# Splitting a depthwise convolution over three engines: one of its four channel tiles goes from VectorE to ScalarE and GpSimd

## The chip, the cores and the metric

One core of a Trainium2 chip runs the whole program in one launch. The metric is the device time of that core in microseconds (us), lower is better. A time is the median of several executions; a profile is one execution.

## What is computed

Two transformer-like layers over 128 context tokens and 256 latent tokens, held together as 384 columns. A layer normalises its input, multiplies it by one wide input projection, runs three token mixers on the result (a gated linear attention, a convolution module, a differential attention), merges them and runs a feed-forward part. The convolution module is the part that the change touches:

```
a, gate = jnp.split(u, 2, axis=-1)
y = a * jax.nn.sigmoid(gate)
y = lax.conv_general_dilated(y, w[:, None, :], window_strides=(1,), padding=[(CONV_PAD, CONV_PAD)],
                             dimension_numbers=('NWC', 'WIO', 'NWC'), feature_group_count=CONV_CH) + b
return jax.nn.silu(layernorm(y, ln_g, ln_b))
```

It has 512 channels and 31 taps a channel, and the layer norm behind it needs the sum over all channels.

## The kernel before

Every array is laid with channels on the 128 partitions and tokens along the free axis. All products with weights run on TensorE in three passes: a float32 weight tile is split into a high half (`w_hi`) and a remainder (`w_lo`), the activations likewise, and each tile takes high by high, high by low and low by high (L834 to L836). The weights come in pieces of 128 x 1024 values, 144 a layer; the input projection has pieces 0 to 57. For each piece SP (the queue that issues the loads) starts a load into `w_raw`, which has two buffers; ScalarE writes the high half (L1356), GpSimd subtracts and writes the low half (L703), and TensorE uses both. ScalarE's high half of piece s waits until TensorE is through with piece s-4, so ScalarE and GpSimd run up to four pieces ahead of it.

Each engine executes its instructions in the order in which they are written, and semaphores tie the engines together. There is no scheduler: what an engine does between two pieces is set by tables of piece numbers at the head of the file. `LEVEL_AT` gives the pieces behind which TensorE computes the seven doubling levels (0 to 6) and the two whole-tile rounds of the linear attention; `EXP_AT` the steps at which ScalarE exponentiates their factors; `SCORE_AT` the pieces behind which it does the scores of the twelve units (head, query tile) of the differential attention, unit 10 behind piece 51. `GATE_AT` and `EARLY_AT` place small products of the modulation vectors (L747) among layer 0's pieces.

For one level i VectorE builds the exponents (L1916 to L1921), copies the result of level i-2 out of PSUM under a mask in the middle of that (L1947), and, once ScalarE has exponentiated, multiplies (L1937). TensorE's level i (L940) needs the multiplication of i and the copy of level i-1, which stands in the build of i+1.

The convolution is done in float32 as 31 taps times four channel tiles (`CT` = 4), 124 instructions a layer, all on VectorE: tap w of tile ct is one 128 x 399 instruction `conv_acc = conv_in * cw + conv_acc` (L1803), where `conv_in` is read at an offset of w columns; the first tap of a tile has no accumulator to read (L1805). They have no place of their own. They are handed out as fillers by further tables: `LEVEL_TAPS` taps before the multiplication of each level from 2 on, `STATE_TAPS` and `OUT_TAPS` around the output of the linear attention, and in the differential attention `MAX_TAPS[u]` taps behind the row minimum of unit u and `WEIGHT_TAPS[u]` behind its weights. In unit 10 VectorE does all taps that are left, and then `conv_total`: three additions of the four tiles (L2022, L2024). Behind piece 53 TensorE sums that over the channels (`conv_mean`, L1094), before the values, transposes and scores that are next, and before piece 54. With the table of before, two taps are left when unit 10 begins, in either layer.

Of the kernel before, what the change touches and what calls it, by code (L numbers as in the profile page):

```python
# [28 lines left out]
P = 128  # L29
D = 1024  # L30
# [67 lines left out]
SECOND_LOAD = [1, 1, 1, 1, 1, 1, 1, 1]  # L98
SECOND_AT = [-1, -1, -1, 99, 99, 99, 99, 99]
GATE_LOAD = [5, 5, 5, 5, 6, 7, 8, 8]  # L100
GATE_AT = [5, 6, 6, 6, 6, 7, 8, 8]
EARLY_LOAD = [7, 8, 8, 9, 9, 14, 15, 15, 16, 16, 16, 18, 18, 21, 21, 22]
EARLY_AT = [11, 11, 11, 11, 11, 12, 12, 13, 16, 16, 16, 16, 17, 17, 18, 18]
TURN_AT_0 = [10, 16, 21]
TAKE_ACT_0 = [10, 17, 23]
PUT_ACT_0 = [14, 19, 24]
# [13 lines left out]
RSTD_ACT_0 = [34, 35, 36, 37]  # L120
PROMPT_KEYS_ACT_0 = 37
STATE_ACT_0 = 39
GLA_HI_ACT_0 = 42
SCORE_ACT_0 = [38, 39, 41, 43, 44, 46, 48, 49, 51, 53, 55, 57, 59, 61]

LEVEL_TAPS_0 = [0, 2, 8, 7, 4, 7, 7]
STATE_TAPS_0 = 15
OUT_TAPS_0 = [5, 6, 6, 1]
MAX_TAPS_0 = [1, 2, 2, 1, 2, 3, 1, 4, 0, 4, 5, 1]
WEIGHT_TAPS_0 = [2, 5, 3, 0, 6, 3, 2, 5, 6, 2, 6, 8]  # L130
BR0, WO0, FI0, FO0 = N_IN, N_IN + N_BR, N_IN + N_BR + N_WO, N_IN + N_BR + N_WO + N_FI
PIECES = FO0 + N_FO
assert PIECES % SPL == 0 and PIECES % RAW == 0
# [34 lines left out]
DECAY_ACT_1 = 10  # L168
SELF_ACT_1 = 11
TURN_AT_1 = [11]  # L170
TAKE_ACT_1 = [11]
PUT_ACT_1 = [15]
LEVEL_AT_1 = [10, 12, 13, 16, 17, 20, 21, 23, 26]
CACHE_KEYS_AT_1 = 23
ROTATE_AT_1 = [24, 26, 29, 30]
PROMPT_KEYS_AT_1 = 33
# [12 lines left out]
LEVEL_TAPS_1 = [1, 2, 6, 7, 1, 7, 10]  # L189
STATE_TAPS_1 = 16  # L190
OUT_TAPS_1 = [5, 6, 6, 1]
MAX_TAPS_1 = [1, 2, 2, 1, 2, 3, 1, 4, 0, 4, 6, 1]
WEIGHT_TAPS_1 = [2, 5, 3, 0, 6, 3, 2, 5, 6, 2, 6, 8]
# [56 lines left out]
def memory(nc):  # L250
# [104 lines left out]
def program(nc, x_prompt, x_sample, cache_diff_k, cache_diff_v, state_gla, c, c_ctx, w_mod, b_mod, norm1_g, norm2_g,  # L355
# [3 lines left out]
    with ExitStack() as ctx:  # L359
# [59 lines left out]

        pads = signal("pads", 3)  # L420
        y_prompt_ready = signal("y_prompt_ready", 2)
        tap = signal("tap", TAPS * CT)
        mean_done = signal("mean_done")
        centred = signal("centred", CT)
        csq = signal("csq", CT)
# [883 lines left out]
        def _(act):  # L1309
# [40 lines left out]
            for l in range(DEPTH):  # L1350
# [22 lines left out]
                def evacuate(c):  # L1373
# [14 lines left out]
                    elif c in (K_CG, K_CG + 1):  # L1388
                        fn(m["sq" if c == K_CG else "cg2"][:], src, ACT.Sigmoid).then_inc(done, 1)
                    elif c in (K_GG, K_GG + 1):  # L1390
                        if c == K_GG:
                            act.wait_ge(late_used.sem, late_at[l, 2, KD - 1] + 1)
                        fn(m["gg"][:, 2 * (c - K_GG):2 * (c - K_GG) + 2, :], src, ACT.Copy).then_inc(done, 1)
                    elif c in VALUES:
                        dst = m["gv" if c < K_DV else "dv"]
                        if c == K_DV + 1:
                            act.wait_ge(*keys_t.at(l, 1))
                        if VALUES[c]:
                            fn(dst[:, 2, :], ps[:, 2 * PAIR_OF[c], :], ACT.Copy).then_inc(done, 1)
                        else:  # L1400
                            fn(dst[:, 0:2, :], ps[:, 2 * PAIR_OF[c]:2 * PAIR_OF[c] + 2, :], ACT.Copy).then_inc(done, 1)
                    elif c < K_DV:
                        side, ht = (c - K_DQ) // 2, 2 * ((c - K_DQ) % 2)

                        fn(m["dqk"][:, side, ht:ht + 2, :], src, ACT.Copy, scale=1.0 if side else -DK ** -0.5).then_inc(done, 1)
                    else:
                        i = 2 * (c - K_GATE)
                        if i == 0:
                            act.wait_ge(early_used.sem, 2 * KD)
                        if i == 16:  # L1410
                            act.wait_ge(*o_mul.at(l, 2 * H))
                        if i + 1 >= 19:
                            act.wait_ge(*tap.at(l, TAPS * CT))
# [107 lines left out]
                for s in range(SPL, BR0 + 5):  # L1521
# [167 lines left out]
        def _(dve):  # L1689
# [52 lines left out]
            for l in range(DEPTH):  # L1742
# [52 lines left out]

                def taps(n):

                    for i in range(taps_done[0], min(taps_done[0] + n, TAPS * CT)):
                        w, ct = i // CT, i % CT
                        src, acc, wt = m["conv_in"][:, ct, w:w + AW], m["conv_acc"][:, ct, :], m["cw"][:, i:i + 1]  # L1800
                        if w:
                            dve.wait_ge(*tap.at(l, i - CT + 1))
# [3 lines left out]
                    taps_done[0] = min(taps_done[0] + n, TAPS * CT)  # L1806
# [249 lines left out]
                for u, (hh, q) in enumerate(UNITS):  # L2056
# [211 lines left out]
```

## Time and profile before

| | |
|---|---|
| median of 3 executions | 1441.1 us (1439.16 to 1444.92) |
| profiled execution | 1441.68 us, its span 1439.8 us |
| TensorE busy | 1395.1 us, 97% of the span |
| VectorE busy | 896.4 us, 62% |
| ScalarE busy | 603.9 us, 42% |
| GpSimd busy | 565.6 us, 39% |

Read it as a kernel with one full engine and three that prepare its operands. A busy time of VectorE or GpSimd is from start to end of an instruction, so it contains what the instruction waited inside. The granted TensorE clock is 0.992 of full over the span.

### The profile page before, as it was taken

To read this page: it belongs to the slowest core of one execution; us is meant where nothing else is said; L and a number is where in the kernel's file an instruction comes from. 1 tells how busy PE (TensorE), PEld (TensorE's weight loads), DVE (VectorE), ACT (ScalarE), POOL (GpSimd) and SP (SyncE) were. 2 spreads that over 40 slices of the span, in tenths; PEclk is the share of its full clock that TensorE was granted. 3 is DMA by queue.
4 is the path that set the end of the run, shared out by engine and by line. 5 is a ranking of instruction groups with operands and counts; after the bars stand their busy time and mean duration, and the time that the engine had idled before them with its cause. 6 is when DMAs were issued, how large, how long until landed. Compare 5 with 4: busy or idle time off the path is not lost.

```text
span 1439.8 us, 21521 instructions
## 1 busy us (share of the span) xinstructions
PE 1395.1 (97%) x8555; PEld 1315.1 (91%) x8555; DVE 896.4 (62%) x1122; ACT 603.9 (42%) x832; POOL 565.6 (39%) x237
## 2 busy tenths in 40 slices
PE   6999999999999999999999999999999999999998
PEld 3887998999998999999979889899999899999998
DVE  4559977995764488666565899698858432111022
ACT  3553434545734333332236344345464443333231
POOL 1353544444463100000025444444436545555552
PEclk9999999999999999999999999999999999999998
DMA  9865232433542766557424323243336434343441
GB/s 334 290 207 173 85 102 89 118 103 97 181 161 89 245 229 216 188 176 245 154 84 143 95 89 103 80 131 91 102 115 207 138 98 137 126 132 120 130 131 60
DMA packets 159212, 208.60 MB, mean 145 GB/s; under 512 B 9228, under 2 KB 126984, under 8 KB 159112
## 3 DMA queue, kind: packets, MB, share of 16 engines
q1 hardware_dynamic: 158560, 207.00, 44.9%
q8 instruction: 68, 1.11, 0.3%
q10 hardware_dynamic: 552, 0.22, 0.1%
q14 instruction: 32, 0.26, 0.1%
HBM read 204.05 MB, written 3.15 MB: 144 GB/s over the span
## 4 chain that ended last, share of the span: by engine, by line
PE 74%; DVE 11%; ACT 5%; DMA 4%; issue 2%; POOL 2%; SPq 1%; DVEq 0%; ACTq 0%; POOLq 0%
PE ps L834 22%; PE ps L836 21%; PE ps L835 21%; POOL w_lo L703 2%; DMA w_raw<-in_w_in_dram 1%; DVE conv_acc L1803 1%; ACT w_hi L1356 1%; DVE fac L1937 1%; DVE attn L1947 1%; DMA w_raw<-in_w_out_dram 1%; PE ps L1087 1%; PE ps L881 1%; DVE gates L2099 1%; DVE t L1762 1%; PE ps L882 1%
## 5 line engine op out<-in xcount | busy, mean ns | idle before, releaser
L703 POOL TENSOR_TENSOR w_lo<-w_raw,w_hi 128x1024 fp32r<-128x1024 f32 (+1 forms) x229 | 562.1, 2456 | 850.6 <-ACT w_hi L1356 728.5
L834 PE MATMUL ps<-h_hi,w_hi 128*128 128x384 f32 x1600 | 546.5, 342 | 6.5 <-DVE h_lo L1768 3.8
L836 PE MATMUL ps<-h_hi,w_lo 128*128 128x384 f32 x1600 | 535.7, 335 | 0.0
L835 PE MATMUL ps<-h_lo,w_hi 128*128 128x384 f32 x1600 | 535.6, 335 | 0.0
L1356 ACT ACTIVATE w_hi<-w_raw 128x1024 fp32r<-128x1024 f32 x199 | 207.6, 1044 | 434.2 <-PE ps L836 303.7
L834 PEld LDWEIGHTS ps<-h_hi,w_hi 128*128 128x128 f32 x1600 | 300.7, 188 | 21.7 <-issue 10.0
L835 PEld LDWEIGHTS ps<-h_lo,w_hi 128*128 128x128 f32 x1600 | 300.9, 188 | 1.4
L836 PEld LDWEIGHTS ps<-h_hi,w_lo 128*128 128x128 f32 x1600 | 300.8, 188 | 0.0
L1803 DVE SCALAR_TENSOR_TENSOR conv_acc<-conv_in,cw,conv_acc 128x399 f32<-128x399 f32 x240 | 210.7, 940 | 1.8
L1659 ACT ACTIVATE w_hi<-w_raw 128x1024 fp32r<-128x1024 f32 x88 | 93.2, 1061 | 211.4 <-PE ps L836 151.8
L834 PE MATMUL ps<-act_hi,w_hi 128*128 128x384 f32 x352 | 118.4, 336 | 0.0
L836 PE MATMUL ps<-act_hi,w_lo 128*128 128x384 f32 x352 | 117.6, 334 | 0.0
L835 PE MATMUL ps<-act_lo,w_hi 128*128 128x384 f32 x352 | 117.6, 334 | 0.0
L2139 DVE TENSOR_TENSOR w_lo<-w_raw,w_hi 128x1024 fp32r<-128x1024 f32 x59 | 72.2, 1224 | 64.1 <-ACT w_hi L1659 39.2
L2153 DVE TENSOR_TENSOR sq<-sq,ps 128x768 f32<-128x768 f32 x22 | 21.0, 952 | 141.7 <-PE ps L836 130.6
L1785 DVE SCALAR_TENSOR_TENSOR x<-ps,mod,x 128x128 f32<-128x128 f32 x32 | 11.2, 350 | 94.6 <-PE ps L836 94.5
L2128 DVE SCALAR_TENSOR_TENSOR mod_acc<-mod_late,cond,mod_acc 128x1024 f32<-128x1024 f32 x56 | 69.3, 1279 | 0.0
L834 PEld LDWEIGHTS ps<-act_hi,w_hi 128*128 128x128 f32 x352 | 66.1, 188 | 1.0 <-issue 0.8
L835 PEld LDWEIGHTS ps<-act_lo,w_hi 128*128 128x128 f32 x352 | 66.1, 188 | 0.1
L836 PEld LDWEIGHTS ps<-act_hi,w_lo 128*128 128x128 f32 x352 | 66.1, 188 | 0.0
L2156 DVE TENSOR_TENSOR act_lo<-sq,act_hi 128x768 fp32r<-128x768 f32 x22 | 38.5, 1751 | 13.6 <-ACT act_hi L1666 13.6
L881 PE MATMUL ps<-w_hi,h_hi 128*128 128x512 f32 x96 | 40.8, 425 | 3.1 <-DVE conv_in L1863 3.1
(262 smaller groups left out, 1656.4 us busy)
## 6 DMA issues: line engine op xcount, KB each, us to landing
w_raw<-in_w_in_dram SPq DMA_DIRECT2D x112, 512.0 KB, 3.6
w_raw<-in_w_ffn_in_dram SPq DMA_DIRECT2D x88, 512.0 KB, 3.5
mod_late<-in_w_mod_dram SPq DMA_DIRECT2D x71, 512.0 KB, 5.3
w_raw<-in_w_ffn_out_dram SPq DMA_DIRECT2D x44, 512.0 KB, 3.7
w_raw<-in_w_branch_dram SPq DMA_DIRECT2D x24, 512.0 KB, 3.4
mod_early<-in_w_mod_dram SPq DMA_DIRECT2D x16, 512.0 KB, 6.6
w_raw<-in_w_out_dram SPq DMA_DIRECT2D x16, 512.0 KB, 3.4
mod_second<-in_w_mod_dram SPq DMA_DIRECT2D x9, 512.0 KB, 11.1
```

The lines of the kernel that those rows point to most:

```text
L703: nc.gpsimd.tensor_tensor(m["w_lo"][:, n % SPL, cols], m["w_raw"][:, n % RAW, cols], m["w_hi"][:, n % SPL, cols].bitcast(F32), ALU.subtrac ...
L834: mm(out, hi[:, at:at + P], rhs[0][:, k, :], start=start, stop=False)
L835: mm(out, hi[:, at:at + P], rhs[1][:, k, :], start=False, stop=False)
L836: ins = mm(out, lo[:, at:at + P], rhs[0][:, k, :], start=False, stop=stop)
L881: mm(o, x[0], w[0], start=k == 0, stop=False)
L1356: fn(m["w_hi"][:, s % SPL, cols], m["w_raw"][:, s % RAW, cols], ACT.Copy).then_inc(hi_ready.sem, 1)
L1659: fn(m["w_hi"][:, s % SPL, :], m["w_raw"][:, s % RAW, :], ACT.Copy).then_inc(hi_ready.sem, 1)
L1803: v.scalar_tensor_tensor(acc, src, wt, acc, ALU.mult, ALU.add).then_inc(tap.sem, 1)
L2128: ins = v.scalar_tensor_tensor(acc, w, by, acc, ALU.mult, ALU.add)
L2139: v.tensor_tensor(m["w_lo"][:, s % SPL, :], m["w_raw"][:, s % RAW, :], m["w_hi"][:, s % SPL, :].bitcast(F32), ALU.subtract).then_inc(lo_re ...
L2153: v.tensor_tensor(m["sq"][:], m["sq"][:], pair[1], ALU.mult).then_inc(u_v.sem, 1)
L2156: v.tensor_tensor(m["act_lo"][:, 2 * i:2 * i + 2, :], m["sq"][:], m["act_hi"][:, 2 * i:2 * i + 2, :].bitcast(F32), ALU.subtract).then_inc( ...
```

## The change

The last channel tile (`VT` = 3) leaves VectorE. ScalarE multiplies tap w of it, behind the high half of piece 19 + w, into one of two new 128 x 399 buffers, `weighted`; GpSimd adds that to `conv_acc` behind the low half of piece 19 + w, for w from 1 to 30. The first tap ScalarE writes into `conv_acc` directly. VectorE keeps 31 taps of three tiles, 93 instead of 124 a layer, and its tables of taps hold smaller numbers. `conv_total` waits for GpSimd's last addition too. A few placements move: one modulation product of layer 0 from behind piece 5 to behind piece 6, two more one piece later, level 6 of layer 1 from behind piece 21 to behind piece 22, one read-out of ScalarE in layer 1 one step earlier, one copy of layer 0 one step earlier. The two buffers overlay columns of `gates` that are free until the gate chunks are read out, and ScalarE waits for the last addition before it writes there.

```diff
-GATE_AT = [5, 6, 6, 6, 6, 7, 8, 8]
+GATE_AT = [6, 6, 6, 6, 6, 7, 8, 8]
-EARLY_AT = [11, 11, 11, 11, 11, 12, 12, 13, 16, 16, 16, 16, 17, 17, 18, 18]
+EARLY_AT = [11, 11, 11, 11, 11, 12, 13, 13, 16, 16, 16, 16, 17, 17, 17, 18]
-GLA_HI_ACT_0 = 42
+GLA_HI_ACT_0 = 41
-LEVEL_TAPS_0 = [0, 2, 8, 7, 4, 7, 7]
+LEVEL_TAPS_0 = [0, 3, 5, 5, 3, 5, 5]
...
-MAX_TAPS_0 = [1, 2, 2, 1, 2, 3, 1, 4, 0, 4, 5, 1]
-WEIGHT_TAPS_0 = [2, 5, 3, 0, 6, 3, 2, 5, 6, 2, 6, 8]
+MAX_TAPS_0 = [1, 1, 1, 1, 2, 2, 0, 3, 0, 3, 3, 1]
+WEIGHT_TAPS_0 = [0, 4, 2, 0, 4, 2, 1, 4, 4, 1, 5, 5]
...
+TAP_FROM = 20
+VT = CT - 1
...
-LEVEL_AT_1 = [10, 12, 13, 16, 17, 20, 21, 23, 26]
+LEVEL_AT_1 = [10, 12, 13, 16, 17, 20, 22, 23, 26]
...
                 low(n)
+                w, layer = n % PIECES - TAP_FROM + 1, n // PIECES
+                if 1 <= w < TAPS:
+                    pool.wait_ge(*weighted.at(layer, w + 1))
+                    if w > 1:
+                        pool.wait_ge(*tap_p.at(layer, w - 1))
+                    acc = m["conv_acc"][:, VT, :]
+                    nc.gpsimd.tensor_tensor(acc, acc, m["weighted"][:, w % 2, :], ALU.add).then_inc(tap_p.sem, 1)
...
+                    w = s - TAP_FROM + 1
+                    if 0 <= w < TAPS:
+                        y = m["conv_in"][:, VT, w:w + AW]
+                        if w == 0:
+                            act.wait_ge(*evacuated(l, K_CA + 1))
+                            fn(m["conv_acc"][:, VT, :], y, ACT.Identity, bias=m["prm"][:, R_CB + VT:R_CB + VT + 1],
+                               scale=m["cw"][:, VT:VT + 1]).then_inc(weighted.sem, 1)
+                        else:
+                            if w >= 3:
+                                act.wait_ge(*tap_p.at(l, w - 2))
+                            fn(m["weighted"][:, w % 2, :], y, ACT.Copy, scale=m["cw"][:, w * CT + VT:w * CT + VT + 1]
+                               ).then_inc(weighted.sem, 1)
...
-                    for i in range(taps_done[0], min(taps_done[0] + n, TAPS * CT)):
-                        w, ct = i // CT, i % CT
+                    for i in range(taps_done[0], min(taps_done[0] + n, TAPS * VT)):
+                        w, ct = i // VT, i % VT
...
-                    dve.wait_ge(*tap.at(l, TAPS * CT))
+                    dve.wait_ge(*tap.at(l, TAPS * VT))
+                    dve.wait_ge(*tap_p.at(l, TAPS - 1))
```

GpSimd, from the first pieces of layer 0 on, before the change:

```order
L703 TENSOR_TENSOR w_lo<-w_raw,w_hi 128x1024 x2
L703 TENSOR_TENSOR w_lo<-w_raw,w_hi 128x128 x2
L703 TENSOR_TENSOR w_lo<-w_raw,w_hi 128x1024 x83
L703 TENSOR_TENSOR w_lo<-w_raw,w_hi 128x128 x2
L703 TENSOR_TENSOR w_lo<-w_raw,w_hi 128x1024 x140
```

The same place with the change, where L711 is the low half and L726 the new addition:

```order
L711 TENSOR_TENSOR w_lo<-w_raw,w_hi 128x1024 x2
L711 TENSOR_TENSOR w_lo<-w_raw,w_hi 128x128 x2
L711 TENSOR_TENSOR w_lo<-w_raw,w_hi 128x1024 x17
L726 TENSOR_TENSOR conv_acc<-conv_acc,weighted 128x399
L711 TENSOR_TENSOR w_lo<-w_raw,w_hi 128x1024
L726 TENSOR_TENSOR conv_acc<-conv_acc,weighted 128x399
```

From piece 20 to piece 49 of either layer an addition of 128 x 399 now stands between two low halves, 30 a layer.

VectorE ahead of level 4 of layer 1 (the factors are `fac`), before the change:

```order
L1921 TENSOR_TENSOR fac_75<-prefix 128x24x16
L1805 TENSOR_SCALAR conv_acc<-conv_in,cw,prm 128x399
L1803 SCALAR_TENSOR_TENSOR conv_acc<-conv_in,cw,conv_acc 128x399 x5
L1937 TENSOR_TENSOR fac_75<-fac_75,gqk 128x1536
L1916 TENSOR_TENSOR fac_77<-prefix 128x12x32
L1947 COPY_PREDICATED attn<-masks,ps 128x512 x3
```

and with it:

```order
L1950 TENSOR_TENSOR fac_75<-prefix 128x24x16
L1834 TENSOR_SCALAR conv_acc<-conv_in,cw,prm 128x399
L1832 SCALAR_TENSOR_TENSOR conv_acc<-conv_in,cw,conv_acc 128x399 x3
L1966 TENSOR_TENSOR fac_75<-fac_75,gqk 128x1536
L1945 TENSOR_TENSOR fac_77<-prefix 128x12x32
L1976 COPY_PREDICATED attn<-masks,ps 128x512 x3
```

Two taps are gone from between the build and the multiplication; the rest is as it was.

VectorE in unit 10 of layer 0, from its row minimum (`mx`) to `conv_total` (`t`), before the change:

```order
L2059 TENSOR_REDUCE mx<-ps 128x2
L1803 SCALAR_TENSOR_TENSOR conv_acc<-conv_in,cw,conv_acc 128x399 x2
L2062 RECIPROCAL mx<-mx 128x2
L2063 TENSOR_SCALAR mx<-mx,lam_120 128x1
L2065 TENSOR_SCALAR prob<-prob,mx 128x384
L2066 SCALAR_TENSOR_TENSOR prob<-prob,mx 128x384
L2022 TENSOR_TENSOR t<-conv_acc 128x399
L2024 TENSOR_TENSOR t<-t,conv_acc 128x399 x2
```

and with it:

```order
L2089 TENSOR_REDUCE mx<-ps 128x2
L1832 SCALAR_TENSOR_TENSOR conv_acc<-conv_in,cw,conv_acc 128x399 x3
L2092 RECIPROCAL mx<-mx 128x2
L2093 TENSOR_SCALAR mx<-mx,lam_121 128x1
L2095 TENSOR_SCALAR prob<-prob,mx 128x384
L2096 SCALAR_TENSOR_TENSOR prob<-prob,mx 128x384
L1832 SCALAR_TENSOR_TENSOR conv_acc<-conv_in,cw,conv_acc 128x399 x5
L2052 TENSOR_TENSOR t<-conv_acc 128x399
L2054 TENSOR_TENSOR t<-t,conv_acc 128x399 x2
```

Eight taps instead of two stand in this stretch. In layer 1 it is four behind the minimum and two behind the weights, six instead of two.

## Rows read from the trace of the kernel before

**Rows 1.** The page's first part: busy time of TensorE and VectorE
```profile
PE 1395.1 (97%) x8555; PEld 1315.1 (91%) x8555; DVE 896.4 (62%) x1122; ACT 603.9 (42%) x832; POOL 565.6 (39%) x237
```
**Rows 2.** Waits of TensorE: us in total, times, longest
```profile
PE ps L940 <- DVE attn L1947: 6.9, 3, 2.7
...
PE ps L881 <- DVE conv_in L1863: 3.1, 1, 3.1
PE ps L1099 <- DVE sq L2030: 2.5, 2, 1.2
...
PE ps L747 <- DMA mod_early<-in_w_mod_dram: 1.1, 1, 1.1
```
**Rows 3.** Stretch of layer 1's levels: PE, PEld, DVE, ACT, POOL busy, clock
```profile
821.00:860.00 39.00, 36.27 (x242) 32.69 (x241) 38.79 (x49) 16.20 (x20) 18.03 (x8) 0.96 0.32 95
```
**Rows 4.** Groups by line and shape, of VectorE, GpSimd and ScalarE
```profile
L1803 DVE SCALAR_TENSOR_TENSOR conv_acc<-conv_in,cw,conv_acc 128x399 f32<-128x399 f32 x240 | 210.7, 940 | 1.8
...
L715 POOL TENSOR_TENSOR xg<-x,prm 128x384 f32<-128x384 f32 x4 | 3.3, 828 | 13.5 <-DVE x L1787 13.5
L703 POOL TENSOR_TENSOR w_lo<-w_raw,w_hi 128x128 fp32r<-128x128 f32 x4 | 2.0, 504 | 19.2 <-ACT w_hi L1356 19.2
...
L1604 ACT ACTIVATE conv_q<-conv_acc 128x399 f32<-128x399 f32 x6 | 3.2, 540 | 0.3
```
**Rows 5.** Line L1803 alone (min/median/max ns), and six taps in a row
```profile
L1803 DVE SCALAR_TENSOR_TENSOR conv_acc<-conv_in,cw,conv_acc x240: 619/629/2819, 126.0 to 1026.7; 128x399 f32<-128x399 f32 x120
...
222.92 3.36 DVE L1803 SCALAR_TENSOR_TENSOR conv_acc<-conv_in,cw,conv_acc 128x399 f32<-128x399 f32 x6
```
**Rows 6.** Timeline ahead of level 4, layer 1: start, us, engine, line
```profile
825.12 7.09 DVE L1803 SCALAR_TENSOR_TENSOR conv_acc<-conv_in,cw,conv_acc 128x399 f32<-128x399 f32 x5
...
828.97 1.47 ACT L1437 ACTIVATE fac<-fac 128x1536 f32<-128x1536 f32 x1
...
829.21 2.58 POOL L703 TENSOR_TENSOR w_lo<-w_raw,w_hi 128x1024 fp32r<-128x1024 f32 x1 [1.21 <-ACT w_hi L1356]
...
832.13 1.75 DVE L1937 TENSOR_TENSOR fac<-fac,gqk 128x1536 f32<-128x1536 f32 x1
...
834.39 1.95 DVE L1947 COPY_PREDICATED attn<-masks,ps 128x512 f32<-128x512 uint8 x3
...
836.49 2.73 PE L940 MATMUL ps<-fac 64*128 64x128 f32 x24 [2.73 <-DVE attn L1947]
```
**Rows 7.** Timeline ahead of level 6, layer 0
```profile
159.03 1.97 DVE L1947 COPY_PREDICATED attn<-masks,ps 128x512 f32<-128x512 uint8 x3
...
161.15 1.61 PE L940 MATMUL ps<-fac 64*128 64x128 f32 x24 [1.46 <-DVE attn L1947]
```
**Rows 8.** The chain that ended last, layer 0 behind piece 5
```profile
56.37 0.57 PE ps L747 x8
```
**Rows 9.** Timeline of unit 10, layer 0: VectorE, GpSimd, TensorE
```profile
327.96 1.97 DVE L1803 SCALAR_TENSOR_TENSOR conv_acc<-conv_in,cw,conv_acc 128x399 f32<-128x399 f32 x2
...
332.01 3.41 DVE L2024 TENSOR_TENSOR t<-t,conv_acc 128x399 f32<-128x399 f32 x2
...
332.57 2.41 POOL L703 TENSOR_TENSOR w_lo<-w_raw,w_hi 128x1024 fp32r<-128x1024 f32 x1 [3.63 <-ACT w_hi L1356]
337.40 2.37 POOL L703 TENSOR_TENSOR w_lo<-w_raw,w_hi 128x1024 fp32r<-128x1024 f32 x1 [2.42 <-ACT w_hi L1356]
...
335.95 0.83 PE L1094 MATMUL ps<-t,ones 128*128 128x399 f32 x2
```
**Rows 10.** The same place in layer 1
```profile
1029.44 3.41 DVE L2024 TENSOR_TENSOR t<-t,conv_acc 128x399 f32<-128x399 f32 x2
...
1033.38 0.83 PE L1094 MATMUL ps<-t,ones 128*128 128x399 f32 x2
```
**Rows 11.** Timeline of unit 3, layer 0: weights done, and their transpose
```profile
267.05 0.35 DVE L2066 SCALAR_TENSOR_TENSOR prob<-prob,mx 128x128 f32<-128x128 f32 x1
...
268.53 0.27 PE L1072 MATMUL ps<-ident,prob 128*128 128x128 f32 x1
```

More of the change, by code:

```diff
@@ L122 @@
 STATE_ACT_0 = 39
-GLA_HI_ACT_0 = 42
+GLA_HI_ACT_0 = 41
 SCORE_ACT_0 = [38, 39, 41, 43, 44, 46, 48, 49, 51, 53, 55, 57, 59, 61]
-LEVEL_TAPS_0 = [0, 2, 8, 7, 4, 7, 7]
-STATE_TAPS_0 = 15
-OUT_TAPS_0 = [5, 6, 6, 1]
-MAX_TAPS_0 = [1, 2, 2, 1, 2, 3, 1, 4, 0, 4, 5, 1]
-WEIGHT_TAPS_0 = [2, 5, 3, 0, 6, 3, 2, 5, 6, 2, 6, 8]
+LEVEL_TAPS_0 = [0, 3, 5, 5, 3, 5, 5]
+STATE_TAPS_0 = 10
+OUT_TAPS_0 = [4, 4, 4, 1]
+MAX_TAPS_0 = [1, 1, 1, 1, 2, 2, 0, 3, 0, 3, 3, 1]
+WEIGHT_TAPS_0 = [0, 4, 2, 0, 4, 2, 1, 4, 4, 1, 5, 5]
 BR0, WO0, FI0, FO0 = N_IN, N_IN + N_BR, N_IN + N_BR + N_WO, N_IN + N_BR + N_WO + N_FI
@@ L170 @@
 TURN_AT_1 = [11]
-TAKE_ACT_1 = [11]
+TAKE_ACT_1 = [10]
 PUT_ACT_1 = [15]
-LEVEL_AT_1 = [10, 12, 13, 16, 17, 20, 21, 23, 26]
+LEVEL_AT_1 = [10, 12, 13, 16, 17, 20, 22, 23, 26]
 CACHE_KEYS_AT_1 = 23
@@ L188 @@
 SCORE_ACT_1 = [38, 39, 41, 43, 44, 46, 48, 49, 51, 53, 55, 57, 59, 61]
[L189 to L193, printed above, removed]
+LEVEL_TAPS_1 = [1, 1, 4, 5, 1, 5, 6]
+STATE_TAPS_1 = 11
+OUT_TAPS_1 = [4, 4, 4, 1]
+MAX_TAPS_1 = [1, 1, 3, 1, 1, 2, 1, 3, 0, 3, 4, 1]
+WEIGHT_TAPS_1 = [1, 4, 2, 0, 4, 2, 2, 3, 4, 2, 4, 6]
 HEAD_SUM_AT_1 = [41, 46, 52]
@@ L316, in memory @@
     over("mod_early", [P, EARLY, D], gates)
+    over("weighted", [P, 2, AW], gates + EARLY * D * 4)
+    assert EARLY * D + 2 * AW <= 16 * T
     assert EARLY * D * 4 <= 16 * T * 4
@@ L421, in program @@
         y_prompt_ready = signal("y_prompt_ready", 2)
-        tap = signal("tap", TAPS * CT)
+        tap = signal("tap", TAPS * VT)
+        weighted = signal("weighted", TAPS)
+        tap_p = signal("tap_p", TAPS - 1)
         mean_done = signal("mean_done")
@@ L1412, in evacuate @@
                         if i + 1 >= 19:
-                            act.wait_ge(*tap.at(l, TAPS * CT))
+                            act.wait_ge(*tap.at(l, TAPS * VT))
+                        if i == 12:
+                            act.wait_ge(*tap_p.at(l, TAPS - 1))
                         fn(m["gates"][:, i:i + 2, :], src, ACT.Copy).then_inc(done, 1)
@@ L1796, in taps @@
                 def taps(n):
-                    for i in range(taps_done[0], min(taps_done[0] + n, TAPS * CT)):
-                        w, ct = i // CT, i % CT
-                        src, acc, wt = m["conv_in"][:, ct, w:w + AW], m["conv_acc"][:, ct, :], m["cw"][:, i:i + 1]
+                    for i in range(taps_done[0], min(taps_done[0] + n, TAPS * VT)):
+                        w, ct = i // VT, i % VT
+                        src, acc, wt = m["conv_in"][:, ct, w:w + AW], m["conv_acc"][:, ct, :], m["cw"][:, w * CT + ct:w * CT + ct + 1]
                         if w:
-                            dve.wait_ge(*tap.at(l, i - CT + 1))
+                            dve.wait_ge(*tap.at(l, i - VT + 1))
                             v.scalar_tensor_tensor(acc, src, wt, acc, ALU.mult, ALU.add).then_inc(tap.sem, 1)
@@ L1805, in taps @@
                             v.tensor_scalar(acc, src, wt, column(R_CB + ct), ALU.mult, ALU.add).then_inc(tap.sem, 1)
[L1806 removed]
+                    taps_done[0] = min(taps_done[0] + n, TAPS * VT)
                 def small_columns(layer):
@@ L2070, in _ @@
                         attention_gain(u // 3 - 2)
-                    taps(WEIGHT_TAPS[l][u] if u < CONV_SUM_UNIT else TAPS * CT)
+                    taps(WEIGHT_TAPS[l][u] if u < CONV_SUM_UNIT else TAPS * VT)
                     if u == CONV_SUM_UNIT:
```

## The prediction

> **What bounds the kernel now.** I read the page's first part before anything else: TensorE is busy 97% of the span, VectorE 62% [rows 1]. So the change relieves an engine that is not the bound, and it can pay only where TensorE waits for that engine. The waits of TensorE tell how much that is: 6.9 us in three waits of a level (L940) for VectorE's masked copy, the longest 2.7; 3.1 once for `conv_in`; 2.5 in two waits of the variance sum [rows 2]. The `conv_in` wait ends before VectorE has done a tap, and the variance sum comes after the last one, so neither can shrink by fewer taps. What taps can influence is the 6.9 us. Each of the two long ones has a second price: level 4 of layer 1 takes 2.73 us after its wait [rows 6], level 6 of layer 0 takes 1.61 [rows 7], both 24 records of the same shape. The stretch round the first has a mean granted clock of 0.96 [rows 3], so part of it ran at the lower of the two levels (1.2 GHz of 2.4). A wait of 2.7 us thus brought 1.1 us more, one of 1.46 us nothing. In the attention part (units 0 to 11) TensorE has no wait for VectorE in the list at all.
>
> **What a tap costs, and what an addition on GpSimd costs.** The mean of a tap is 940 ns [rows 4], but that is no price: the median is 629, the longest 2819, and six in a row take 3.36 us, 0.56 each [rows 5]. The rest is waiting inside the instruction. Where it comes from is seen ahead of level 4: five taps take 7.09 us in which GpSimd's low half (2.58 us) falls, and VectorE's multiplication starts within 0.35 us after that low half ends [rows 6]. In unit 10 two additions of two operands take 3.41 us round a low half of 2.41 [rows 9]. So a VectorE instruction that reads two SBUF operands stands still while GpSimd works, and moving a tap saves VectorE 0.56 us, not 0.94.
>
> The addition that takes its place isn't in the trace. Below it stands GpSimd's 128 x 384 product, 828 ns, one operand of which is a repeated column: 0.86 us for 399. Above, a line through 504 ns for 128 columns [rows 4] and 2.41 us for 1024 [rows 9] gives 1.08. Both operands are whole tiles, as in the low half, so I take 1.07. Per layer VectorE gives up 31 x 0.56 = 17 us and GpSimd gains 30 x 1.07 = 32 us of work in which VectorE may stand still. Whether VectorE comes out ahead depends on how often it wants to start something during an addition; in the dense stretches it is busy 38.8 us of 39 [rows 3], so nearly always.
>
> The Trainium skill (page "SBUF — State Buffer", section "Who interferes with whom") says that a VectorE instruction with two SBUF inputs and a GpSimd instruction that reads SBUF exclude one another for the whole instruction. The trace agrees, with the numbers above. By that rule the change costs VectorE up to 32 - 17 = 15 us a layer instead of saving it 17; the sum below takes, place by place, what the rows show.
>
> **The change part by part,** against the profiled execution's 1441.68 us.
>
> *ScalarE's 31 weightings a layer*: some 0.54 us each (its square of a 128 x 399 tile [rows 4]). Behind each are queued the exponentials of a level and, four pieces later, the high halves. ScalarE writes high halves four pieces ahead and is busy 42%, so the halves are covered: 0. Without that cover it would be 31 x 0.54 = 17 us a layer. The exponential of a level gets 0.54 us later; ahead of level 4 it ends at 830.4 and the multiplication starts at 832.13 [rows 6], which covers it.
>
> *The modulation product of layer 0* that moves behind piece 6: 0.57 us on the chain that ended last, ahead of the decay's products [rows 8]. It moves behind them: -0.6. Its load and SP's order stay. The two others: the 1.1 us wait for their load [rows 2] may go, but the 3.1 us wait for `conv_in` follows two pieces later and ends when VectorE is ready, whenever TensorE comes. It takes back what the first gives: 0.
>
> *Level 6 of layer 0*, now 1.46 us late behind VectorE's copy that ends at 161.0 [rows 7]. The tables give five taps less from level 2 to 6 (21 to 16): -2.8 us. Four additions fall in, for pieces 20 to 23: at most +4.3, at least 0 if each falls into VectorE's reads of PSUM. I take 3.7, since VectorE has no idle time there. Net +0.9. Bounds: -1.46 (the wait can't be less than nothing) and +1.5.
>
> *Level 4 of layer 1*. Two taps fewer, -1.1; but the multiplication can't start before the low half of 829.21 ends at 831.8 [rows 6], so only 0.35 is gained there, and the addition for piece 20 follows this low half and holds up either the multiplication or the build behind it: +1.07. Net +0.8. Bounds: -3.8 (wait and lower clock gone) and +1.1.
>
> *Units 0 to 9 of the attention*: 18 taps fewer in layer 0 (54 to 36), 16 additions more for pieces 34 to 49. VectorE has some time between units, and TensorE's transpose comes 1.1 us after the weights are done even where they are due soonest [rows 11]: one addition on that path fits. 0.
>
> *Unit 10 and `conv_total`*. This is the term that decides. In layer 0 the last addition of `conv_total` ends at 332.01 + 3.41 = 335.42, and TensorE's sum over channels starts at 335.95 [rows 9]: slack 0.53 us. In layer 1 it is 1032.85 and 1033.38, 0.53 again [rows 10]. When unit 10 starts is set by TensorE (its scores), and so is the sum's place, so the distance is the same after the change; taps done faster before unit 10 can't help, because their number per unit is fixed by the table. In this stretch stand eight taps instead of two in layer 0, six instead of two in layer 1.
> - Layer 0: six more taps, 3.4 us, less the slack: 2.9 us of waiting. That is the lower bound. Upper: `conv_total` then reaches past 337.40, where the next low half begins [rows 9], and is held 2.1 us more: 5.0. I take 4.0. It is longer than 2.7 us, so the lower clock comes too, 1.1 as at level 4, partly inside the wait: +1.0. Together 5.0.
> - Layer 1: four more taps, 2.2 us, less 0.53: +1.7, ending before its next low half; +0.1 for the way low halves fall, 1.8. Too short for the clock.
> What follows (scores of unit 11, centring, squares) is tied to TensorE's sum and moves with it, so nothing is caught up. Late next is piece 54 and all behind it.
>
> Sum: -0.6 + 0.9 + 0.8 + 4.0 + 1.0 + 1.8 = +7.9, so 1449.6 for an execution like the profiled one. That one was 0.6 above the median of 1441.1: **1449.0**.
>
> **The rivals.**
> - *The relief wins.* VectorE's late copies are early enough: levels 6 and 4 lose their waits (-1.46 - 2.73 - 1.1), the product gives -0.6, and unit 10 costs its lower bounds (2.9 + 1.7, no clock). Sum -1.3: 1439.8. For it: fewer taps stand before both levels. Against it: GpSimd's additions start exactly there. It decides if an addition holds VectorE less than 0.56 us on the mean. Not slower. Chance 0.28.
> - *The additions cascade.* In the units whose transpose comes one piece after the scores, the slack is 1.1 us [rows 11]; two additions or a displaced low half on that path (2 x 1.07) exceed it by 1.0, in three units of each layer: 6 us more, 1455. For it: VectorE is dense. Against: TensorE has no wait there now. Chance 0.14.
> - *Weights arrive late.* If GpSimd's low halves slip behind additions, the load of the next piece but one slips too. Low half and addition take 2.41 + 1.07 = 3.5 us, and a piece takes over 4 us of TensorE (levels of neighbouring pieces), so it fits on the mean; if it fails by 0.15 us a piece in 60 pieces: 9 us more, 1458. Chance 0.08.
>
> The forecast has 0.50.
>
> **How the numbers follow.** A measurement of this kernel can tell some 0.5%, 7.2 us: faster is below 1433.9, slower above 1448.3. The forecast's own range is 1444 to 1453, 0.6 of it above 1448.3: 0.31. The other two slow cases give 0.20. The relief case lies within 0.5%, with a tail beyond (0.07 with what I haven't thought of). The range goes from the relief's 1440 to the cascade's 1455, which leaves out half of each tail, 0.2.
>
> **What would show it.** L1094's wait for VectorE's last addition of `conv_total` (L2054), absent now, of 3 to 5 us in layer 0 and about 1.8 in layer 1; level 4 of layer 1 still waiting near 3 us; a mean tap that is no shorter than 940 ns by more than a few per cent, though a quarter of the taps is gone; GpSimd's addition at 1.07 us or more. I am wrong if L1094 shows no wait (then the stretch behaves otherwise than its count of taps), if the additions last well below 0.8 us, or if TensorE waits for `w_lo`.

## The result, and the profile after

The changed kernel takes 1457.66 us (median of 4, 1452.10 to 1460.76) against 1441.36 of before (median of 4 in the same comparison, 1439.16 to 1444.92): ratio 1.0098 [1.0078, 1.0117], 1% slower. A later comparison (experiment 5) gives 1.0109 [1.0092, 1.0125]. The direction was forecast, the size was not: 1449 had been predicted, and 1455 was the top of the range.

First the busy times of the changed kernel, beside [rows 1]:

```profile
PE 1401.5 (96%) x8555; PEld 1320.4 (91%) x8555; DVE 854.2 (59%) x1060; ACT 635.5 (44%) x894; POOL 634.2 (44%) x297
```

VectorE lost 42 us of busy time, GpSimd gained 69, ScalarE 32. TensorE has the same 8555 products and is busy 6.4 us longer, so part of the loss lies inside its products: a lower clock. The waits of TensorE of the changed kernel (us in total, times, longest), beside [rows 2]:

```profile
PE ps L955 <- DVE attn L1976: 8.1, 4, 2.7
PE ps L1109 <- DVE t L2054: 6.3, 2, 4.7
...
PE ps L987 <- DVE stateT L2022: 1.9, 2, 1.0
...
PE ps L980 <- DVE attn L1976: 0.9, 1, 0.9
...
PE ps L896 <- DVE conv_in L1892: 0.4, 1, 0.4
```

L1109 is the sum over channels, `conv_mean`. It had no wait before and has 6.3 us now. L987 transposes the state of the linear attention behind its whole-tile rounds (L980). The wait of the rounds is new; that of the transposes was 0.3 us once before and is 1.0 us in either layer now. The taps and what took their place, by line and shape:

```profile
L1832 DVE SCALAR_TENSOR_TENSOR conv_acc<-conv_in,cw,conv_acc 128x399 f32<-128x399 f32 x180 | 168.3, 991 | 1.8
L726 POOL TENSOR_TENSOR conv_acc<-conv_acc,weighted 128x399 f32<-128x399 f32 x60 | 72.6, 1209 | 0.0
L1561 ACT ACTIVATE weighted<-conv_in,cw 128x399 f32<-128x399 f32 x60 | 37.0, 617 | 0.0
```

The mean tap went from 940 ns [rows 4] to 991: each tap that is left waits longer.

Where the time went is seen by putting the start of the same product in both traces side by side. In layer 0 of before, the transpose of the state starts at 188.21 without a wait. Ahead of it VectorE multiplies the whole-tile factors (`fac`), rotates queries (`dqk`, three instructions), writes `q_enter` and copies the state. The timeline of before:

```profile
177.49 1.42 DVE L1935 TENSOR_TENSOR fac<-fac,gqk 128x512 f32<-128x512 f32 x2 [2.46 <-ACT fac L1427]
...
179.68 2.58 DVE L1956 TENSOR_TENSOR dqk<-dqk,rope 128x512 f32<-128x512 f32 x1
...
183.01 3.48 DVE L1984 TENSOR_SCALAR q_enter<-fac,etot 128x128 f32<-128x128 f32 x4
...
188.21 0.44 PE L972 MATMUL ps<-ident,fac 128*128 128x128 f32 x2
```

The same place in the changed kernel:

```profile
176.62 0.63 ACT L1561 ACTIVATE weighted<-conv_in,cw 128x399 f32<-128x399 f32 x1
...
177.66 1.27 ACT L1444 ACTIVATE fac<-prefix,ltot 128x128 f32<-128x128 f32 x4
...
178.96 4.00 DVE L1964 TENSOR_TENSOR fac<-fac,gqk 128x512 f32<-128x512 f32 x2 [3.28 <-ACT fac L1444]
...
180.02 2.39 POOL L711 TENSOR_TENSOR w_lo<-w_raw,w_hi 128x1024 fp32r<-128x1024 f32 x1 [0.46 <-ACT w_hi L1371]
...
182.37 1.34 POOL L726 TENSOR_TENSOR conv_acc<-conv_acc,weighted 128x399 f32<-128x399 f32 x1
...
183.73 0.69 DVE L1985 TENSOR_TENSOR dqk<-dqk,rope 128x512 f32<-128x512 f32 x1
...
185.18 3.91 DVE L2013 TENSOR_SCALAR q_enter<-fac,etot 128x128 f32<-128x128 f32 x4
189.73 0.41 DVE L2022 COPY stateT<-ps 128x256 f32<-128x256 f32 x1
...
190.20 0.44 PE L987 MATMUL ps<-ident,fac 128*128 128x128 f32 x2 [0.97 <-DVE stateT L2022]
```

The multiplication takes 4.00 us instead of 1.42, round a low half with its addition. Most of that is no loss: before, the same low half fell into the rotation (2.58 us, now 0.69). Three smaller terms add up:

- ScalarE's exponentials stand behind a weighting now, and end 3.95 us after their high half starts, where it was 3.43: 0.52 us.
- From the start of the multiplication to that of `q_enter` it was 5.52 us and is 6.22: 0.70 us, with GpSimd's additions in it.
- `q_enter` takes 3.91 us instead of 3.48: 0.43 us.

Together VectorE's copy of the state is 1.65 us later, measured against TensorE. There was 0.67 us of slack, so TensorE waits 0.97. The change does take two taps off VectorE ahead of the multiplication (four in layer 1), but there VectorE only waits longer for the exponentials (3.28 us instead of 2.46), so nothing pays for the lateness. The transpose comes 1.99 us later than before (188.21 to 190.20): 1.0 of it is the new wait, the rest came earlier. Behind this wait the clock is low. The stretch from 190.1 us of the changed kernel (PE, PEld, DVE, ACT, POOL busy, clock):

```profile
190.10:194.50 4.40, 4.30 (x16) 4.07 (x16) 3.43 (x7) 0.00 (x0) 2.23 (x2) 0.61 0.44 133
```

That costs another 1.6 us here (the next rotation product is 3.57 us later than before). The sum over channels of unit 10, layer 0, in the timeline of the changed kernel, beside [rows 9]:

```profile
331.54 2.53 DVE L1832 SCALAR_TENSOR_TENSOR conv_acc<-conv_in,cw,conv_acc 128x399 f32<-128x399 f32 x3
...
335.54 4.96 DVE L1832 SCALAR_TENSOR_TENSOR conv_acc<-conv_in,cw,conv_acc 128x399 f32<-128x399 f32 x5
...
336.15 2.83 POOL L711 TENSOR_TENSOR w_lo<-w_raw,w_hi 128x1024 fp32r<-128x1024 f32 x1 [3.60 <-ACT w_hi L1371]
...
340.98 2.34 POOL L711 TENSOR_TENSOR w_lo<-w_raw,w_hi 128x1024 fp32r<-128x1024 f32 x1 [2.00 <-ACT w_hi L1371]
...
341.14 3.22 DVE L2054 TENSOR_TENSOR t<-t,conv_acc 128x399 f32<-128x399 f32 x2
...
344.42 1.61 PE L1109 MATMUL ps<-t,ones 128*128 128x399 f32 x2 [4.73 <-DVE t L2054]
```

Two low halves fall into the stretch. The five taps stand round the first, the last additions round the second, as was argued for the upper bound. The product itself takes 1.61 us, where it took 0.83 [rows 9], and what follows is slow too; by the last score product of unit 11 that has given another 1.7. Layer 1 [rows 10] has the wait in its shorter form:

```profile
1048.25 0.94 PE L1109 MATMUL ps<-t,ones 128*128 128x399 f32 x2 [1.61 <-DVE t L2054]
```

Added up over the profiled executions (1455.74 against 1441.68, +14.1):

- up to level 6 of layer 0: +1.0. Contained in it are a `conv_in` wait that was 2.7 us shorter and a lower clock behind it that is absent (1.4 us); that wait ends when VectorE is ready, so it takes up what TensorE lost before it (the last section tells of it);
- from there to behind the state's transposes: +2.6 (1.03 to the transpose, 1.58 behind it);
- units 0 to 9: 0; unit 10: +4.9 and +1.7;
- layer 1's levels: -0.3; its whole-tile rounds, the state and the clock behind: +3.1; unit 10: +1.8;
- the rest: -0.8.

Unit 10 is 8.4 of 14.1, the whole-tile rounds and the state 5.8.

### The profile page after: what moved, and what is told of

The parts are those of the page before. It is cut to its first block, busy times and chain, and to the rows that moved or that the text cites. A ratio compares the mean times of both kernels' runs of the same rounds, so it can differ in the third digit from the quotient of the medians.

```text
span 1453.9 us, 21643 instructions
## 1 busy us (share of the span) xinstructions
PE 1401.5 (96%) x8555; PEld 1320.4 (91%) x8555; DVE 854.2 (59%) x1060; ACT 635.5 (44%) x894; POOL 634.2 (44%) x297
## 4 chain that ended last, share of the span: by engine, by line
PE 73%; DVE 12%; ACT 5%; DMA 5%; POOL 2%; issue 2%; SPq 1%; DVEq 0%; POOLq 0%; ACTq 0%
PE ps L849 21%; PE ps L850 20%; PE ps L851 20%; DMA w_raw<-in_w_in_dram 2%; POOL w_lo L711 2%; DVE conv_acc L1832 2%; ACT w_hi L1371 1%; DVE attn L1976 1%; DVE fac L1966 1%; DMA w_raw<-in_w_out_dram 1%; PE ps L896 1%; PE ps L898 1%; PE ps L897 1%; PE ps L1102 1%; DVE gates L2129 1%
## 5 line engine op out<-in xcount | busy, mean ns | idle before, releaser
L711 POOL TENSOR_TENSOR w_lo<-w_raw,w_hi 128x1024 fp32r<-128x1024 f32 (+1 forms) x229 | 560.6, 2450 | 797.0 <-ACT w_hi L1371 675.0
L1832 DVE SCALAR_TENSOR_TENSOR conv_acc<-conv_in,cw,conv_acc 128x399 f32<-128x399 f32 x180 | 168.3, 991 | 1.8
L726 POOL TENSOR_TENSOR conv_acc<-conv_acc,weighted 128x399 f32<-128x399 f32 x60 | 72.6, 1209 | 0.0
```

What stands on the lines that cost most here:

```text
L726: nc.gpsimd.tensor_tensor(acc, acc, m["weighted"][:, w % 2, :], ALU.add).then_inc(tap_p.sem, 1)
```

## The experiments

Ratios are to the kernel before, on the same chip. Where a kernel is said to differ from "changed" or from "before", the edit is all that differs.

**1. The changed kernel, with two taps left at unit 10.**

```diff
-OUT_TAPS_0 = [4, 4, 4, 1]
+OUT_TAPS_0 = [6, 6, 6, 1]
-OUT_TAPS_1 = [4, 4, 4, 1]
+OUT_TAPS_1 = [5, 6, 5, 1]
```

> The changed kernel, with six more VectorE taps in the output part of layer 0's linear attention and five more in layer 1's (OUT_TAPS 6,6,6,1 and 5,6,5,1), where VectorE idles for ScalarE, so that at most two are left at unit 10, as before the change. Count theory (the waits of the sum over channels come from the number of taps left at unit 10): both waits of L1109 go, with the lower clock behind the first, 4.7 + 1.7 + 1.8 = 8.2 us less than the changed kernel's profiled 1455.7: near 1447.5. Rival (GpSimd's additions make VectorE late, and the lateness only shows there): the waits stay or move to another unit, and the time stays within 2 us of the changed kernel.

The kernel before took 1445.21 us on the chip of experiments 1 to 4, 4 us more than the 1441.4 that the expectations count from, so the ratios are to be compared. Measured: 1445.9 us, 1.0014 [1.0000, 1.0029]. L1109 is gone from the waits; the rest of the loss stays. Waits of TensorE:

```profile
PE ps L955 <- DVE attn L1976: 8.1, 4, 2.7
...
PE ps L987 <- DVE stateT L2022: 1.9, 2, 1.0
```

The result is 2 us above the kernel before, where the trace of the changed kernel left 5.7 outside unit 10 (14.1 less 8.4); experiment 10 repeats this version on another chip and finds 6. Either way the entries of `OUT_TAPS` are most of the loss. (The expectation speaks of five more taps in layer 1; the edit gives four, which is what brings six down to two.)

**2. The changed kernel without GpSimd's additions.** The fourth tile stays incomplete; the semaphore is only counted up.

```diff
-                    acc = m["conv_acc"][:, VT, :]
-                    nc.gpsimd.tensor_tensor(acc, acc, m["weighted"][:, w % 2, :], ALU.add).then_inc(tap_p.sem, 1)
+                    pool.sem_inc(tap_p.sem, 1)
```

> The changed kernel without GpSimd's 60 additions: it leaves the fourth tile's convolution incomplete; GpSimd still waits for ScalarE and signals, but touches no memory. Count theory: the waits of unit 10 stay (4.7 and 1.6, no addition runs then), and what goes is what the additions hold up: the waits and the lower clock at the whole-tile rounds, 2.6 in layer 0 and 3.2 in layer 1, and 1 to 3 us at the levels: 1447 to 1450. Rival (the additions make VectorE late everywhere): all goes, 1441 or less.

Measured: 1449.56 us, 1.0034 [1.0017, 1.0051]. The waits of TensorE:

```profile
PE ps L1108 <- DVE t L2053: 6.3, 2, 4.7
...
PE ps L954 <- DVE attn L1975: 4.8, 2, 2.7
```

The wait at unit 10 is the same to a tenth, so it has nothing to do with the additions. The wait for the state (1.9 us) is absent, so that one needs them.

**3. The kernel before, with eight and six taps left at unit 10.** No ScalarE weighting, no addition, all 124 taps on VectorE.

```diff
-OUT_TAPS_0 = [5, 6, 6, 1]
+OUT_TAPS_0 = [3, 4, 4, 1]
-OUT_TAPS_1 = [5, 6, 6, 1]
+OUT_TAPS_1 = [4, 5, 4, 1]
```

> The kernel before, with nothing on ScalarE and GpSimd, but six taps fewer in layer 0's output part and four fewer in layer 1's (OUT_TAPS 3,4,4,1 and 4,5,4,1), so that eight and six are left at unit 10, as in the changed kernel. Count theory: TensorE waits about 4.7 and 1.6 us for the sum and gets the lower clock once: 1441.4 + 8 = 1449. Rival: VectorE has them done in time since no addition holds it: within 2 us of 1441.

Measured: 1455.16 us, 1.0063 [1.0039, 1.0087]. The product and its wait in layer 0:

```profile
340.22 1.70 PE L1094 MATMUL ps<-t,ones 128*128 128x399 f32 x2 [4.73 <-DVE t L2024]
```

4.73 us, the very wait of the changed kernel. The table of taps alone makes a kernel without the split 0.6% (9 us) slower.

**4. The kernel before, with only the moved placements** (one modulation product, two `EARLY_AT` entries, level 6 of layer 1, two steps of ScalarE).

> The kernel before with only the placement moves of the change (modulation products, level 6 of layer 1 one piece later, the read-out and the copy one step earlier). My prediction's step: 0.6 us less, 1440.8. Rival: the moves lengthen the way to level 0, whose wait rose from 1.5 to 2.7 us, but the wait for conv_in takes that back: 1441.4, no difference. A difference over 2 us would say that the moves carry part of the loss.

Measured: 1445.11 us, 1.0006 [0.9985, 1.0027]. The placements carry nothing that can be measured. These four ran on one chip.

**5. The changed kernel again,** as the reference of a second chip, on which experiments 6 to 8 ran too.

> The changed kernel once more, unaltered, beside the three others on one chip. It was 0.98% slower in 4 runs. If that holds, 1.0098 within its interval; the other three runs of this call are read against this one. If unit 10's 8.4 us and the additions' 5.8 are all there is, some 14 us above the kernel before.

Measured: 1456.6 us, 1.0109 [1.0092, 1.0125]. The waits at unit 10 are 4.73 and 1.60 us again, those for the state 0.98 and 0.97. But behind the first of these the clock is full this time, and the whole-tile rounds and the state cost 4.2 us instead of 5.8.

**6. Both edits: two taps left at unit 10 and no additions** (the fourth tile incomplete, as in 2).

> Both repairs together: the taps of unit 10 moved ahead as in the first experiment, and GpSimd's additions left out (the fourth tile's convolution is incomplete). Count theory plus lock theory: TensorE waits for neither the sum nor the whole-tile rounds, what is left are the waits for the levels, as before: within 1.5 us of the kernel before, 1.000. Rival (the 60 weightings on ScalarE cost something of their own): 3 us or more above it.

Measured: 1437.89 us, 0.9970 [0.9956, 0.9985]. Both new waits are absent. This is faster than before and than expected (within 1.5 us of it), with all of ScalarE's weightings in it: without the additions no new wait shows that could come from them. 31 taps fewer a layer on VectorE would be worth 0.3%, 4 us, if GpSimd had nothing to do for it.

**7. The kernel before, plus additions on spare tiles.** GpSimd does 30 additions of 128 x 399 a layer at the places of the change, on tiles that nobody reads. VectorE keeps all 124 taps.

```diff
+                w, layer = n % PIECES - 19, n // PIECES
...
+                if 1 <= w < TAPS:
+                    pool.wait_ge(*spare_p.at(layer, w + 1))
+                    acc = m["spare"][:, 0, :]
+                    nc.gpsimd.tensor_tensor(acc, acc, m["spare"][:, 1, :], ALU.add).then_inc(spare_p.sem, 1)
```

> The kernel before with all its 124 taps on VectorE, and 30 additions of 128 x 399 a layer on GpSimd behind the same low halves as in the change, on two spare tiles that nobody reads (a memset of each ahead of them). Lock theory: VectorE loses about as much as it waits for in 60 x 1.2 us, and has no relief; its waits at levels, whole-tile rounds and the sum over channels all appear: 8 to 20 us slower, and the mean tap rises above 1 us. Rival (additions only fill GpSimd's idle time): within 2 us of the kernel before.

Measured: 1471.38 us, 1.0212 [1.0193, 1.0230], the slowest of all, 29 us where 8 to 20 had been expected. Its busy times, and the waits of TensorE for VectorE:

```profile
PE 1407.3 (95%) x8555; PEld 1324.8 (90%) x8555; DVE 933.7 (63%) x1122; ACT 603.5 (41%) x832; POOL 649.2 (44%) x301
...
PE ps L950 <- DVE attn L1959: 12.1, 5, 3.1
PE ps L1082 <- DVE prob L2078: 5.9, 4, 2.5
```

VectorE's instructions are the same 1122 as before, and it is busy 37 us longer (933.7 against 896.4) [rows 1]. Here the attention units' transposes (L1082) wait for VectorE's weights, which happens in no version with 93 taps. The 60 additions thus cost by what else VectorE has to do: 29 us with 124 taps on VectorE, 6 to 11 with 93 (by the ratios of experiments 1 and 6, and of 2 and 5).

This run also has the additions without ScalarE's weightings. The transpose of the state in layer 0:

```profile
197.68 0.44 PE L982 MATMUL ps<-ident,fac 128*128 128x128 f32 x2 [0.34 <-DVE stateT L2005]
```

It waits 0.34 us instead of 0.97, and the clock stays full. The 124 taps don't matter here, since VectorE waits 1.97 us for the exponentials behind them. So the additions alone give a third of this wait, and the rest comes with the weighting in front of the exponentials. (Layer 1 can't be compared: TensorE has waited 2.89 us there shortly before, ahead of a whole-tile round.)

**8. A later split.** VectorE keeps the first eight taps of the fourth tile, GpSimd's 23 additions a layer stand behind pieces 28 to 50, and the extra taps are given to `OUT_TAPS`.

```diff
-STATE_TAPS_0 = 10
-OUT_TAPS_0 = [4, 4, 4, 1]
+STATE_TAPS_0 = 13
+OUT_TAPS_0 = [7, 8, 8, 1]
...
+KEEP, TAP_AT = 8, 28
...
-                w, layer = n % PIECES - TAP_FROM + 1, n // PIECES
-                if 1 <= w < TAPS:
+                w, layer = n % PIECES - TAP_AT, n // PIECES
+                if 0 <= w < MOVED:
```

> An attempt at a better split: VectorE keeps the first 8 taps of the fourth tile, ScalarE and GpSimd do the other 23 behind pieces 28 to 50, so that no addition runs in the levels or the whole-tile rounds; VectorE's taps stand where it idles (OUT_TAPS 7,8,8,1), two left at unit 10 in layer 0, none in layer 1. If additions in the levels and rounds are what the first experiment still loses: 2 to 5 us less than that one (1.0014), so 0.998 to 1.0 of the kernel before. Rival: additions in the attention units cost as much, 1.0014 or more.

Measured: 1455.46 us, 1.0104 [1.0076, 1.0133]. The expectation fell. There is no wait for the state any more, as expected, though one of 0.80 us ahead of a whole-tile round of layer 1 stays. No addition has run in that layer by then, so the additions alone don't make that wait, though experiments 2 and 6 lack it; what makes it is open. And there is a new wait, larger than what was saved. VectorE ahead of it, and TensorE's scores of unit 0:

```profile
231.50 10.09 DVE L1835 SCALAR_TENSOR_TENSOR conv_acc<-conv_in,cw,conv_acc 128x399 f32<-128x399 f32 x8
...
242.76 0.80 PE L1077 MATMUL ps<-dqk 64*128 64x128 f32 x4 [5.95 <-DVE gg L2046]
```

Eight fillers that should cost 8 x 0.56 = 4.5 us took 10.09, since two low halves and two additions of GpSimd fell into them. Behind them stood the multiplication of the linear attention's output (L2046), for which unit 0 waits: 5.95 us in layer 0 and as much again in layer 1 (11.9 in all).

**9. The same later split, with its taps given out evenly.** Two are left at unit 10.

```diff
-LEVEL_TAPS_0 = [0, 3, 5, 5, 3, 5, 5]
+LEVEL_TAPS_0 = [0, 3, 6, 6, 4, 6, 6]
-OUT_TAPS_0 = [7, 8, 8, 1]
+OUT_TAPS_0 = [6, 6, 6, 1]
-LEVEL_TAPS_1 = [1, 1, 4, 5, 1, 5, 6]
-STATE_TAPS_1 = 14
-OUT_TAPS_1 = [7, 8, 8, 1]
+LEVEL_TAPS_1 = [1, 1, 4, 6, 2, 6, 7]
+STATE_TAPS_1 = 13
+OUT_TAPS_1 = [6, 6, 6, 1]
```

> The version with additions only from piece 28 on, its taps given out so that two are left when unit 10 begins and none of the fillers ahead of unit 0 grows beyond what the fixed tables of the first experiment had. If the additions of pieces 20 to 27 are what made VectorE late in the levels and whole-tile rounds, and the surplus of fillers was what made the scores of unit 0 wait, then the waits of TensorE for the linear attention's state, for unit 0's scores and for the sum over channels are all absent, and the time is 0.996 to 1.000 of before, 2 to 5 us under the version that only gives the taps out otherwise. The rival, that the attention units pay for the additions that remain (22 a layer), gives 1.001 to 1.004.

Measured: 1444.8 us, 0.9998 [0.9977, 1.0019]. There is no wait for the state, none for unit 0's scores and none for the sum over channels. The state's transpose comes without a wait, and the clock is full behind it; timeline, and the stretch around it with the columns as above:

```profile
193.02 0.44 PE L993 MATMUL ps<-ident,fac 128*128 128x128 f32 x2
...
190.00:200.00 10.00, 9.94 (x58) 9.28 (x57) 8.81 (x15) 2.97 (x4) 6.09 (x5) 1.00 0.38 107
```

**10. Experiment 1 again, beside experiment 9 on the same (third) chip.**

> The changed kernel with two taps left at unit 10, run again beside the version above on the same chip: 1.000 to 1.003 of before, with TensorE's waits for the state (1.9 us in two) and the lower clock behind them still there. If it comes out under the version above, additions in the levels are not what is left of the loss.

Measured: 1451.41 us, 1.0042 [1.0021, 1.0063], somewhat over its expectation. It has the 1.9 us wait for the state, as in 1, but not the lower clock that had been expected behind it:

```profile
195.50 0.44 PE L987 MATMUL ps<-ident,fac 128*128 128x128 f32 x2 [0.96 <-DVE stateT L2022]
...
195.40:199.80 4.40, 4.30 (x25) 4.20 (x26) 3.85 (x8) 0.00 (x0) 2.23 (x2) 1.00 0.50 149
```

The later split is 6.6 us faster by the medians, and the two intervals do not touch. It equals the kernel before and doesn't beat it. No version with the additions did.

## Why the prediction was wrong

- *What bounds the kernel* held. The losses at unit 10 and at the state are waits of TensorE for VectorE, or a low clock behind one.
- *Unit 10 and `conv_total`* held as a mechanism, down to the line named and the second low half. "I take 4.0" measured 4.73 against bounds of 2.9 and 5.0; "+1.0" for the clock measured 1.7; "1.8" in layer 1 measured 1.76. Together 8.4 instead of 6.8 (8.7 in experiment 3, 9.4 in experiment 5). Experiments 1 and 3 show it from both sides.
- **The step that failed is the missing term.** The sum jumps from the levels to "Units 0 to 9 of the attention" and leaves out what lies between: the whole-tile rounds, the state and its transposes. Additions for pieces 20 to 49 fall there too, and the taps taken away ahead of the two multiplications give nothing back, since VectorE waits for ScalarE's exponentials behind them. It measured 2.6 us in layer 0 and 3.1 in layer 1, 5.8 in all by the unrounded figures; in the profiled executions of experiments 5, 1 and 10 it was 4.2, 4.2 and 2.7, since the lower clock did not follow each wait. Experiment 2 takes the additions away and the wait with them, and 7, which has additions and no weightings, shows a third of the wait in layer 0. In 9 neither a weighting stands in front of the whole-tile exponentials nor an addition beside the multiplication behind them; the multiplication takes 1.42 us in layer 0 as before, and the wait is absent, though two additions follow before the transposes.
- *Level 6 of layer 0*: the wait went from 1.46 [rows 7] to 1.74, +0.3 of the +0.9 taken. *Level 4 of layer 1*: the wait is 2.65, where 2.73 [rows 6] + 0.8 had been forecast. The mechanism given there held, and both sizes were off. The timeline of the changed kernel, on ScalarE, VectorE, GpSimd and TensorE:

```profile
839.37 2.40 POOL L711 TENSOR_TENSOR w_lo<-w_raw,w_hi 128x1024 fp32r<-128x1024 f32 x1 [1.42 <-ACT w_hi L1371]
...
839.66 1.47 ACT L1454 ACTIVATE fac<-fac 128x1536 f32<-128x1536 f32 x1
...
841.16 2.23 DVE L1966 TENSOR_TENSOR fac<-fac,gqk 128x1536 f32<-128x1536 f32 x1 [2.23 <-ACT fac L1454]
...
841.72 2.42 POOL L726 TENSOR_TENSOR conv_acc<-conv_acc,weighted 128x399 f32<-128x399 f32 x1
...
846.57 2.93 PE L955 MATMUL ps<-fac 64*128 64x128 f32 x24 [2.65 <-DVE attn L1976]
```

  VectorE is through with its three taps and sits idle 2.23 us for ScalarE's exponential. But the exponential isn't the end of it: the multiplication then takes 2.23 us instead of 1.75 and ends 1.62 us after the low half. Experiment 9 has no weighting and no addition here, so its exponential comes earlier against the low half:

```profile
835.14 2.40 POOL L715 TENSOR_TENSOR w_lo<-w_raw,w_hi 128x1024 fp32r<-128x1024 f32 x1 [1.65 <-ACT w_hi L1377]
...
836.40 2.75 DVE L1969 TENSOR_TENSOR fac<-fac,gqk 128x1536 f32<-128x1536 f32 x1 [1.94 <-ACT fac L1460]
```

  Its multiplication again ends 1.61 us after the low half (1.62 in experiment 6), and the wait of TensorE is 2.06, as it is in experiments 2 and 6 (weighting, no addition). So the low half holds the multiplication, as the prediction said; the two taps give 0.67 us (0.35 had been taken) and the addition costs 0.59 (1.07 had been taken). The first rival counted on 2.73 here and on 1.46 at level 6 of layer 0; without any addition (experiment 6) the waits shrink by 0.67 and 0.54 only. The third wait of a level in [rows 2], the 2.7 us in layer 1 ahead of this one, is 2.71 or 2.72 in the profile of every version: no tap and no addition moves it.
- *Two readings.* Ahead of level 4 two low halves fall into the five taps of 7.09 us, not one; the earlier starts at 825.13 and takes 2.86. And of "the two others", which the section on the change puts one piece later, one moves a piece later and one a piece earlier (18 to 17). Neither changes the sum.
- *An addition, "I take 1.07"*: it measured 1209 ns in the mean. The one above took 2.42 us, while VectorE's multiplication (841.16 to 843.39) was under way: GpSimd waits for VectorE as VectorE for GpSimd. With the additions left out and the same table of taps, the mean tap falls to 910 ns (experiment 6) from 989 (experiment 1). The Trainium skill (page "SBUF — State Buffer", section "Who interferes with whom") lets the two engines exclude one another; the runs agree that they do, but the 15 us a layer that the prediction made of it as an upper end came to 6 to 11 for both layers in time. That only what hits a late place counts is how I read it.
- *The modulation product, -0.6, with the two others*: experiment 4 shows no difference. *ScalarE's weightings, 0*: true of experiment 6, without the additions. In the changed kernel the weighting puts the whole-tile exponentials 0.52 us later, on the path of the state (experiment 7 against the changed kernel).
- *The additions cascade* (through the attention units) fell for this kernel: its transposes show no wait. Experiment 7 shows the mechanism at work with 124 taps on VectorE. *Weights arrive late* fell: no wait for `w_lo` is in the list. *The relief wins* is the direction that experiment 6 shows (4 us), for a kernel without the additions and with two taps left at unit 10.
- The gap is 8.7 us (1457.66 against 1449.0). 6.2 of it is in the sum: 5.8 of the missing term and 1.6 of unit 10, less 1.2 elsewhere. The rest lies in executions: the profiled one of the changed kernel is 1.9 us under its median, and that of before was 0.6 over the median that the forecast took off.

## What to carry to other kernels

Where fillers (here the taps) are handed out by a table, count what is left for the last place that must take "all the rest": here smaller entries left four and three times the taps there, and this alone was most of the loss. When work is added to an engine that holds up another one, go through every stage that it falls into and not only those in which work is taken away; a stage without relief pays. And look at what comes second at each wait: the time that VectorE won at level 4 went into 2.2 us of waiting for ScalarE's exponential, and the instruction behind that was still held by GpSimd's low half.

## What the runs showed of the hardware

- A wait of 1 us can be followed by the lower clock: 0.97 us ahead of L987 in layer 0 of the changed kernel, then a stretch at 0.61, 1.6 us dearer. The same wait (0.96 to 0.98 us, at the same two places) stands in four profiles, of experiments 1, 5 and 10 beside the changed kernel's. In four of the eight cases the lower clock follows: in both layers of the changed kernel, in layer 0 of experiment 1 and in layer 1 of experiment 5. In experiment 10 it follows neither. Longer waits at full clock stand beside them: 1.74 ahead of level 6 and 2.68 ahead of level 0 in the changed kernel, whose 24 records took the same 1.61 us as before. So the length of the wait doesn't decide, and neither does the place. The rule of thumb in the prediction, 2.7 yes and 1.46 no, was no rule, and what decides is open.
- The wait for `conv_in` (L896) differs between executions of the same kernel: 0.4 us in the profile of the changed kernel, 1.0 in that of its second run; 0.3 and 5.8 in the two runs of the version of experiment 1, whose profiled times were 1446.06 and 1451.40 (on two chips). The twelve times of experiment 9 fall into a group of 1438.0 to 1440.6 and one of 1444.3 to 1448.0, and the profiled one, 1447.99, has a wait of 5.6. That this wait makes the two groups is argued, not shown, and what sets it is open. It is reason enough to take many executions for differences of half a per cent.
